# Rate products ahead of the first recurrence unit, and idle identity products in TensorE's waits

## What is computed

```python
def direction(d, reverse):
    w_log = -jax.nn.softplus(-(w0[d] + tw @ w_up[d])) - 0.5
    decay = jnp.exp(-jnp.exp(w_log))
    a = jax.nn.sigmoid(a0[d] + ad @ a_up[d])          # the "rate"
    kd = k * (1.0 + (a - 1.0) * k_a)
    y = wkv_scan(heads(r), heads(decay), heads(kd), heads(v), kk, heads(a), reverse)
    return y, kd

def step(state, inp):                                  # in wkv_scan
    r_t, w_t, k_t, v_t, kk_t, a_t = inp
    sa = jnp.einsum('bhij,bhj->bhi', state, -kk_t)
    state = (state * w_t[:, :, None, :] + sa[..., :, None] * (kk_t * a_t)[:, :, None, :]
             + v_t[..., :, None] * k_t[:, :, None, :])
    return state, jnp.einsum('bhij,bhj->bhi', state, r_t)

def hier_moe(x, ...):                                  # routing: group, two experts, rank in the expert
    group = jnp.argmax(softmax(x @ wg1 + bg1)); fine = ...
    top_p, top_e = lax.top_k(softmax(fine), 2)
    ...                                                # each expert: silu(xb @ w_gate) * (xb @ w_up) @ w_down
```

## Time and profile before

| | us |
|---|---|
| median of three runs | 1960.43 |
| lowest, highest | 1951.36, 1962.71 |
| the profiled execution, its own time | 1960.83 |
| its span in the trace | 1959.0 |

### The profile page before, as it was taken

One profiled execution on the slowest core, in us unless ns is written; L12 is line 12 of the kernel. 1 busy time (PEld: TensorE's weight loads), 2 busy tenths in 40 slices (PEclk: granted clock), 3 DMA queues, 4 the chain that ended last, 5 costly groups with the idle time before them and its releaser, 6 DMA issues.

```text
span 1959.0 us, 22615 instructions
## 1 busy us (share of the span) xinstructions
PE 1804.3 (92%) x8984; PEld 892.1 (46%) x8984; DVE 676.3 (35%) x1285; ACT 449.8 (23%) x926; POOL 73.6 (4%) x110
## 2 busy tenths in 40 slices
PE   6999789989997999999999989878979999999997
PEld 3434478878644333333333344666543333333332
DVE  3169776776332311111111245673241111111114
ACT  3284422222421111111111132342111111111111
POOL 4120000000000000000000200000000000000002
PEclk9999888998997999999999989887979999999999
DMA  8000000001242799999999972100039999999997
GB/s 290 5 0 1 1 1 1 1 1 44 87 172 86 291 429 430 428 429 429 428 429 429 368 271 86 43 1 1 0 159 368 431 428 428 430 429 429 430 428 274
DMA packets 68230, 460.95 MB, mean 235 GB/s; under 512 B 18700, under 2 KB 19846, under 8 KB 43590
## 3 DMA queue, kind: packets, MB, share of 16 engines
q1 hardware_dynamic: 56118, 435.90, 53.6%
q10 hardware_dynamic: 9744, 15.77, 2.1%
q0 software_dynamic: 2304, 8.39, 1.3%
HBM read 442.21 MB, written 17.83 MB: 235 GB/s over the span
## 4 chain that ended last, share of the span: by engine, by line
PE 81%; DVE 10%; ACT 5%; issue 2%; DMA 2%; SPq 0%; POOL 0%; DVEq 0%; ACTq 0%; POOLq 0%
PE bank L706 21%; PE bank L732 12%; PE bank L680 11%; PE bank L1969 6%; PE bank L929 4%; PE bank L1008 3%; PE bank L2265 3%; PE bank L2105 2%; PE bank L688 2%; ACT hT L458 2%; PE bank L2114 2%; PE bank L2096 1%; PE bank L994 1%; DVE X L1799 1%; PE bank L273 1%
## 5 line engine op out<-in xcount | busy, mean ns | idle before, releaser
L706 PE MATMUL bank<-ring,arena 128*64 128x512 f32 x2048 | 450.4, 592 | 1.6 <-DVE arena L538 1.6
L605 DVE TENSOR_TENSOR arena<-arena,bank 64x512 f32<-64x512 f32 x64 | 68.3, 1067 | 626.0 <-ACT arena L466 626.0
L706 PEld LDWEIGHTS bank<-ring,arena 128*64 128x64 f32 x2048 | 146.8, 137 | 293.4 <-issue 291.3
L680 PE MATMUL bank<-arena 128*64 128x512 f32 x1024 | 235.8, 602 | 7.3 <-DVE arena L605 4.9
L732 PE MATMUL bank<-ring,arena 128*64 128x512 f32 x1024 | 237.4, 606 | 0.9 <-ACT arena L470 0.9
L1969 PE MATMUL bank<-hT,ring 128*128 128x512 f32 x336 | 147.3, 598 | 6.1 <-ACT arena L1418 4.0
L680 PEld LDWEIGHTS bank<-arena 128*64 128x64 f32 x1024 | 74.2, 139 | 156.3 <-issue 129.8
L466 ACT ACTIVATE arena<-bank 64x512 f32<-64x512 f32 x64 | 37.9, 592 | 401.1 <-PE bank L706 401.1
L732 PEld LDWEIGHTS bank<-ring,arena 128*64 128x64 f32 x1024 | 68.6, 138 | 124.3 <-issue 123.1
L538 DVE TENSOR_TENSOR arena<-bank,gffn 128x512 f32<-128x512 f32 x64 | 44.3, 692 | 188.8 <-PE bank L688 188.8
L1969 PEld LDWEIGHTS bank<-hT,ring 128*128 128x128 f32 x336 | 64.1, 192 | 88.0 <-issue 86.5
(11 more groups left out here) (364 smaller groups left out, 1957.9 us busy)
## 6 DMA issues: line engine op xcount, KB each, us to landing
ring<-in_moe_w_gate_dram SPq DMA_DIRECT2D x64, 2048.0 KB, 10.9
ring<-in_moe_w_up_dram SPq DMA_DIRECT2D x64, 2048.0 KB, 15.8
ring<-in_moe_w_down_dram SPq DMA_DIRECT2D x64, 2048.0 KB, 13.1
expert_rows<-arena ACTq DMA_DIRECT2D x120, 128.0 KB, 8.3
ring<-in_rec_w_in_dram SPq DMA_DIRECT2D x5, 2048.0 KB, 12.9
ring<-in_att_w_in_dram SPq DMA_DIRECT2D x3, 2048.0 KB, 8.5
ring<-in_rec_w_out_dram SPq DMA_DIRECT2D x2, 2048.0 KB, 7.9
ring<-in_att_w_out_dram SPq DMA_DIRECT2D x2, 2048.0 KB, 19.8
```

Of the source, the lines that this page charges most:

```text
L605: nc.vector.tensor_tensor(hb[0:CAP, par, :].rearrange("s (f p) -> s p f", f=4), sg[0:CAP, par, :].rearrange("s (p f) -> s p f", f=4), bank ...
L680: mm = nc.tensor.matmul(bank[2][h * CAP:(h + 1) * CAP, :], onehot[:, par, t, :], xm[:, t, h * 512:(h + 1) * 512], start=(t == 0), stop=(t ...
L706: mm = nc.tensor.matmul(bank[par][k * CAP:(k + 1) * CAP, :], xg[:, par, c, :], W[k][:, c * FF:(c + 1) * FF], start=(c == 0), stop=(c == KC ...
```

## The change

- `rate(v)` writes the bank `RATE_BANK[v]` (7, 0, 1, 2, 3, 7, 0 for v = 1 to 7), and all seven are issued between `first_products(0)` and `spread_rows(0)`; only the sixth and the seventh wait for a sigmoid. The six calls inside unit 0 are removed. ScalarE's seven sigmoids stand together ahead of `block_turned(0)`.
- After `spread_rows(0)` TensorE waits for all sigmoids and issues `spin(5, 0)`: five products of the identity with 512 columns of a constant mask into bank 0, whose results nothing reads. `turn_blocks(0)` follows.
- In units 0 to 6, `spin(3, 0)` stands between `t(u, 5)` and `turn_blocks(u + 1)`. The wait of unit 0 for a sigmoid ahead of `spread_rows(1)` is removed.
- `pe_moe` of both layers begins with `fill(4)`: four products of the identity with 512 columns of ones into bank 6, ahead of the wait for `choice_ready`.

```diff
--- before.py
+++ after.py
@@ -344,6 +344,7 @@
             G_A[u], g = g, g + 1
         G_END = g
         KKB = (0, 1, 6, 7)
+        RATE_BANK = (0, 7, 0, 1, 2, 3, 7, 0)
 
         one_col = ones[:, 0:1]
         LOOP_STEPS = 9
@@ -657,8 +658,14 @@
             if t == TT - 1:
                 mm.then_inc(lg_done, 1)
 
+        def fill(n):
+            for _ in range(n):
+                nc.tensor.matmul(bank[6][:, :], ident[:, :], ones[:, :].unsqueeze(1).to_broadcast([P, 4, P]),
+                                 start=True, stop=True)
+
         def pe_moe(pe, l):
             m = moe[l]
+            fill(4)
             pe.wait_ge(choice_ready, l + 1)
             for t in range(TT):
                 o = bank[3][:, t * EXPERTS:(t + 1) * EXPERTS]
@@ -1372,7 +1379,7 @@
             def rate_sigmoid(u):
                 g, c = G_A[u], V_A0 + (u % 2) * FT + u // 2
                 act.wait_ge(gemm_done, g + 1)
-                src = bank[6 + u % 2] if u else bank[2 + g % 4]
+                src = bank[RATE_BANK[u]] if u else bank[2 + g % 4]
                 nc.scalar.activation(asg[:, u, :] if u else asg0, src[:, :], ACT.Sigmoid,
                                      bias=VA[:, c:c + 1]).then_inc(gemm_out, 1)
 
@@ -1532,31 +1539,24 @@
                     exp_factors((u + 1) // 2, (u + 1) % 2)
                 if u:
                     rhs_copy(*prev, 0)
-                else:
-                    rate_sigmoid(2)
-                    rate_sigmoid(3)
                 turned_levels(u, copied(u))
                 if u:
                     u_copy(*prev, 0)
                     output_copies(*prev, 0)
                     rhs_copy(*prev, 1)
-                else:
-                    for v in (4, 5, 6):
-                        rate_sigmoid(v)
                 turned_levels(u, copied(u) + 2)
                 if u:
                     u_copy(*prev, 1)
                     if u == UNITS - 1:
                         gn_square(0)
                     output_copies(*prev, 1)
-                else:
-                    rate_sigmoid(7)
                 if u < UNITS - 1:
                     block_turned(u + 1)
                 else:
                     gn_log(0)
                     gn_exp(0)
-            rate_sigmoid(1)
+            for v in range(1, UNITS):
+                rate_sigmoid(v)
             block_turned(0)
             for u in range(UNITS):
                 unit_copies(u)
@@ -2147,9 +2147,9 @@
                 mm.then_inc(t_done, 1)
 
             def rate(v):
-                if v >= 3:
-                    pe.wait_ge(gemm_out, G_A[v - 2] + 1)
-                low_rank(bank[6 + v % 2][:, :], v, 32)
+                if v >= 6:
+                    pe.wait_ge(gemm_out, G_A[v - 5] + 1)
+                low_rank(bank[RATE_BANK[v]][:, :], v, 32)
 
             def gn_rows(ft):
                 pe.wait_ge(loop_step, LOOP_STEPS * (ft + 1))
@@ -2167,6 +2167,11 @@
             def gn_square(ft):
                 pe.wait_ge(gn_sq, ft + 1)
                 nc.tensor.matmul(bank[gn_bank[ft][0]][:, :], blk[:, :], gn_v[ft], start=True, stop=True).then_inc(gn_var, 1)
+
+            def spin(n, b):
+                for _ in range(n):
+                    nc.tensor.matmul(bank[b][:, :], ident[:, :], chunkmask[:, 0, :, :].rearrange("p a b -> p (a b)"),
+                                     start=True, stop=True)
 
             def unit(u):
                 prev = ((u - 1) // 2, (u - 1) % 2) if u else None
@@ -2175,33 +2180,23 @@
                     last_z(u - 1)
                     turn(*prev)
                     last_t(u - 1)
-                else:
-                    rate(2)
                 rest_products(u, 0)
                 if u:
                     rhs(*prev, 0)
                     pe.wait_ge(t6_out, u)
                 t(u, 3)
-                if u == 0:
-                    rate(3)
                 rest_products(u, 1)
                 turn_level(u, 3)
                 if u:
                     solve(*prev, 0)
-                else:
-                    rate(4)
                 rest_products(u, 2)
                 z(u, 4)
                 if u:
                     outputs(*prev, 0)
-                else:
-                    rate(5)
                 rest_products(u, 3)
                 t(u, 4)
                 if u:
                     rhs(*prev, 1)
-                else:
-                    rate(6)
                 if u < UNITS - 1:
                     first_products(u + 1)
                 else:
@@ -2211,28 +2206,28 @@
                 turn_level(u, 4)
                 if u:
                     solve(*prev, 1)
-                else:
-                    rate(7)
                 z(u, 5)
                 if u:
                     outputs(*prev, 1)
                 if u < UNITS - 1:
-                    if u == 0:
-                        pe.wait_ge(gemm_out, G_A[6] + 1)
                     spread_rows(u + 1)
                 else:
                     gn_gate(0)
                     gn_square(0)
                 t(u, 5)
                 if u < UNITS - 1:
+                    spin(3, 0)
                     turn_blocks(u + 1)
                 turn_last(u)
             pe.sem_inc(ys_out, 1)
             pe.wait_ge(sst_zero, 1)
             first_products(0)
             pe.wait_ge(kk_max, FT)
-            rate(1)
+            for v in range(1, UNITS):
+                rate(v)
             spread_rows(0)
+            pe.wait_ge(gemm_out, G_END)
+            spin(5, 0)
             turn_blocks(0)
             for u in range(UNITS):
                 unit(u)
```

## The result

| | before | after |
|---|---|---|
| median (runs) | 1959.06 us (4) | 1930.61 us (4) |
| lowest, highest | 1951.36, 1962.71 | 1927.72, 1934.45 |
| ratio after/before | | 0.9857, 95% interval 0.9829 to 0.9884 |
| span of the profiled execution | 1959.0 | 1929.5 |
| mean granted clock in it | 0.949 | 0.967 |

What follows compares the result with a forecast made beforehand. TensorE was taken as bound by waits for the DVE between recurrence units and half-clock work behind them. Gains 20.2 + 2.6 + 4.2 + 3.5 = 30.5 us from 1960.8 gave 1930 us, range 1918 to 1946.

Steps and rivals of the forecast that it cites:

- Price of an idle product, and its cover: Each 0.86 us at full clock; three, 2.57 us, fit the 2.39 to 2.60 us wait, with 0.5 us slack in most.
- The transitions: Seven gaps between recurrence units: three idle products in each speed up turn_last, z and last_z, gaining 20.2 us together.
- The upper bound chosen for the unknown: In the seven unit gaps the clock stays at 1.00; the lower bound was a fall as now, gain 0.
- the rival in which it falls anyway: Clock falls between units despite idle products, nothing gets faster there: 1950 us, up to 1958 with slow routing; chance 0.10.
- that in which the idle products run slow: Idle products run at half speed, three taking 5.1 us in a gap of 2.5: 1981 us; chance 0.05.
- The front: Seven rates ahead of unit 0: turn_blocks(0) 1.8 us late, six products leave unit 0, net gain 2.6 us.
- I take 6 us, so 212: Ahead of unit 0, full clock returns 6 us after PE resumes at 205.9, so the rates end at 216.0.
- rates spaced 1.7 us up to the seventh: Sign of a wrong forecast: all seven rates ahead of unit 0 run at half clock, 1.7 us apart.
- The rival of the slow front: 32-row rates do not raise the clock, turn_blocks(0) 7 us later; with no routing gain 1945 us; chance 0.19 jointly.
- The routings: Four idle products ahead of each layer's choice make ranks run at full clock: 4.2 us in layer 0, 3.5 in layer 1.
- The half gather: First gather after the ranks in each layer: half its possible gain counted, 1.5 us in layer 0, 0.8 in layer 1.
- The four terms: Gains of 20.2 us between units, 2.6 ahead of and in unit 0, 4.2 and 3.5 in the layers' routing: 30.5 us.

Runs made afterwards that it cites:

- the routings alone: The kernel before with only the four idle products ahead of the choice in both routings added: 1949.01 us, ratio 0.996 (0.9937 to 0.9983).

## Why the prediction was right, and where it was wrong

- **Price of an idle product, and its cover: right.** The 0.86 us from the earlier trace rows fits the 2.74 us of three with their latency. They hid in the gap, as costed; the slack was 0.8 us and not the 0.5 that was counted.
- **The transitions: right.** 20.4 us between the profiles against 20.2, with turn_last, z and last_z at the lengths taken from the earlier trace rows. The upper bound chosen for the unknown (the clock stays at 1.00) was the right one; the rival in which it falls anyway is out, and that in which the idle products run slow, too. The reason given was only half of it: "PE would be busy for nearly all of the stretch". Busy with 32-row products, the clock falls in five of seven transitions.
- **The front: wrong, by 5 us.** The step that failed is "I take 6 us, so 212" for the clock's return in the rates; it never came back in them, so they ended at 219.84 and not at 216.0, and spread_rows and part of the idle products were slow as well. Turn_blocks(0) came 5.7 us late; the rest of unit 0, from there to the first turn_last, was forecast at 29.2 us and took 28.5. The net is a loss of 2.4 us in place of a gain of 2.6. One of the prediction's own signs of being wrong came up, rates spaced 1.7 us up to the seventh (1.75 here), and first_products of unit 1 came at 241.81 and not near 236.8. The rival of the slow front named this mechanism, with 0.19 for it and a slow routing together, and argued against it that the rate is 512 columns long; it is the rows that count. By the Trainium skill (TensorE: Matmul & The Clock Gate, Why this matters for your kernels) a TensorE kept busy without a break gets to the full level. The trace of after disagrees for 12.24 us of unbroken 32-row products. The same section of the Trainium skill says that a product over 32 rows takes as long as one over 128, and there the trace agrees: 2.84 and 2.74 us for six passes at the full level.
- **The routings: right in sum, not in the parts.** The gathers start 2.9 and 2.6 us sooner, where 2.7 was forecast for each (3.1 from the ranks, less 0.4 for a late start). The half gather, 1.5 and 0.8 us, was a mean over two cases: it came out as 0 and 1.4. In all, 6.9 us between the profiles against 7.7, and 7.8 us by the ratio of the routings alone (0.4% of 1955.7, interval 3.3 to 12.3).
- **The sum came out closer than its terms deserve.** The four terms give 24.9 us (-2.4 + 20.4 + 2.9 + 4.0), by which the time would be 1936 and not 1930; that the sum came out to the microsecond is luck. The profiles add 6.3 us from attention and the end, where the change does nothing (3.0 us of it is a pause of PE ahead of its last products, which before's profile has and after's has not), less 1.7 us for one slow stretch ahead of the output projection. The runs of before lie between 1946 and 1969 us, so differences of this size come and go between executions of one kernel. The 24.9 us of the terms and the 28.45 us of the medians are both within the measured interval (22.7 to 33.5 us), so nothing here needs a further cause.

## What to carry to other kernels

Look behind TensorE's waits as well as at them: here each wait of 2.39 to 3.51 us between units cost its own length and then the half clock behind it. Idle products of full height that just fill the wait gave back 2.9 us at each place, and three more than that, of 2.57 us, cost 1.74 us. Count rows before counting on a busy stretch to raise the clock: a 32-row product whose weights were padded with zero rows to 128 raised the clock here, at the price of a clear and a copy on GpSimd, and unpadded it did not. Where work is pulled forward into one block, ask at which clock the block will run: the rates cost 1.05 us each where they stood, at the full level, and 1.75 in the block.

## What the runs showed that was not expected

PE at 3.00 of 3.00 us busy lost the clock: 1.00 in the first window of the rates, 0.77 and then 0.50 in the next two. Products of as many columns over 128 rows, whose weights were zero in 96 of them (the 512 columns they multiply were full), raised it from 0.56 to 1.00 in the last two of these windows, so zero weights do not keep it down. And a single idle product of full height kept the clock up in five of seven transitions, with 1.53 to 1.75 us of the gap left idle, and not in another with 1.74; three on 32 rows lost it in a transition in which PE stood still nowhere. So the idle time left in a gap decides only in part.
